# Attention's score matmuls: from one sub-head at a time to both sub-heads in turn

## The reference, cut to what matters

```
def one_block(qblk):                                # 128 queries
    s = einsum('bqhad,bkhad->bhaqk', qblk, k) * scale   # a: sub-head 0 or 1, d: 64 features
    p = softmax(s, axis=-1)
    a = p[:, :, 0] - lam * p[:, :, 1]
    return einsum('bhqk,bkhv->bqhv', a, v)
```

## Time and profile before

| | us |
|---|---|
| median of 3 runs | 3460.33 |
| span of the profiled execution, first to last instruction | 3460.0 |
| PE busy in it | 3105.3 (90%) |
| DVE busy | 1429.9 (41%) |
| ACT busy | 847.0 (24%) |
| attention's first score matmul / last take_o | 339.69 / 723.09 |

### The profile page before, as it was taken

The page is one execution under the profiler, slowest core; times in us unless marked ns, Lnnn a source line. Parts: engine busy times, 40 slices in busy tenths (PEclk is TensorE's granted clock), DMA queues, the critical chain, the costliest instruction groups (busy, mean ns, idle before and its releaser), DMA issues. The chain is left out here.

```text
span 3460.0 us, 42215 instructions
## 1 busy us (share of the span) xinstructions
PE 3105.3 (90%) x16350; PEld 2915.4 (84%) x16350; DVE 1429.9 (41%) x3053; ACT 847.0 (24%) x1041; POOL 747.3 (22%) x250
## 2 busy tenths in 40 slices
PE   5897889869699999999959996999779999999995
PEld 4897666649699999999949994788669999999995
DVE  4677555537523232323343335553462223232325
ACT  3301333340611111111050003552242111111113
POOL 1443000031422112112041111221233211221120
PEclk9998666689899999999979997666889999999997
DMA  5232000023111011101024332110411111111101
GB/s 206 80 119 93 0 1 0 0 100 116 73 42 56 36 36 48 36 36 36 0 113 146 120 133 96 48 47 20 146 43 74 37 48 36 39 57 37 36 12 55
DMA packets 54898, 212.86 MB, mean 62 GB/s; under 512 B 6001, under 2 KB 18993, under 8 KB 45489
## 3 DMA queue, kind: packets, MB, share of 16 engines
q1 hardware_dynamic: 52240, 203.61, 16.4%
q10 hardware_dynamic: 2592, 8.38, 0.6%
HBM read 186.80 MB, written 25.17 MB: 61 GB/s over the span
## 5 line engine op out<-in xcount | busy, mean ns | idle before, releaser
L579 PE MATMUL ps<-hh,wi_hi 128*128 128x384 f32 x2112 | 708.9, 336 | 9.2 <-POOL hl L403 4.9
L581 PE MATMUL ps<-hh,wi_lo 128*128 128x384 f32 x2112 | 708.2, 335 | 0.0
L580 PE MATMUL ps<-hl,wi_hi 128*128 128x384 f32 x2112 | 708.1, 335 | 0.0
L579 PE MATMUL ps<-hh,whi 128*128 128x384 f32 x1344 | 459.6, 342 | 59.6 <-POOL wlo L692 33.3
L961 DVE TENSOR_TENSOR hid<-ps,hid 128x384 f32<-128x384 f32 x132 | 73.4, 558 | 1047.0 <-ACT hid L871 1017.7
L580 PE MATMUL ps<-hl,whi 128*128 128x384 f32 x1344 | 457.1, 340 | 0.0
L581 PE MATMUL ps<-hh,wlo 128*128 128x384 f32 x1344 | 456.6, 340 | 0.0
L579 PEld LDWEIGHTS ps<-hh,wi_hi 128*128 128x128 f32 x2112 | 398.6, 189 | 12.9 <-POOL hl L403 5.7
L580 PEld LDWEIGHTS ps<-hl,wi_hi 128*128 128x128 f32 x2112 | 398.5, 189 | 0.0
L581 PEld LDWEIGHTS ps<-hh,wi_lo 128*128 128x128 f32 x2112 | 398.4, 189 | 0.0
L951 DVE SCALAR_TENSOR_TENSOR x<-ps,mod,x 128x128 f32<-128x128 f32 (+1 forms) x704 | 327.3, 513 | 77.6 <-PE ps L581 72.9
(11 more groups left out here) (174 smaller groups left out, 3999.9 us busy)
## 6 DMA issues: line engine op xcount, KB each, us to landing
raw_in<-in_w_ffn_in_dram SPq DMA_DIRECT2D x44, 1024.0 KB, 4.8
wmt<-in_w_mod_t_dram SPq DMA_DIRECT2D x80, 512.0 KB, 3.5
raw_out<-in_w_ffn_out_dram SPq DMA_DIRECT2D x22, 1024.0 KB, 4.7
gla_spill<-turn SPq DMA_DIRECT2D x24, 576.0 KB, 3.0
head<-gla_spill SPq DMA_DIRECT2D x12, 1152.0 KB, 6.7
raw<-in_w_in_odd_dram SPq DMA_DIRECT2D x24, 512.0 KB, 3.7
raw<-in_w_in_even_dram SPq DMA_DIRECT2D x16, 512.0 KB, 5.6
wm<-in_w_mod_dram SPq DMA_DIRECT2D x12, 512.0 KB, 9.1
```

Source lines behind the costliest of these rows:

```text
L579: pe.matmul(acc, w_hi, in_hi, start=first, stop=False)
L580: pe.matmul(acc, w_hi, in_lo, start=False, stop=False)
L581: return pe.matmul(acc, w_lo, in_hi, start=False, stop=last)
```

## The change

PE's order alone is changed. The 18 score matmuls of a block stand together, chunk by chunk and part by part, alternating between sub-head 0 (partitions 0 to 63) and sub-head 1 (64 to 127). They begin when both sub-heads' exponentials of the block before are made, and `scored` goes up by two behind the last. The values and then all three rounds of transposes follow. Nothing is added or left out: each block has the same 18 score matmuls, 9 transposes, maxima, exponentials and copies.

```
-                def scores(i, u, a):
+                def scores(i, u):
...
-                    wait(pe, exped, i, H2, 2 * (u - 1) + a + 1)
+                    wait(pe, exped, i, H2, 2 * u)
                     for c, cols in enumerate(keys):
-                        acc = ps[:, 3 * a + c, 0:cols.stop - cols.start]
-                        pe.matmul(acc, q_hi[rows, q], k_hi[rows, cols], start=True, stop=False)
-                        pe.matmul(acc, q_hi[rows, q], k_lo[rows, cols], start=False, stop=False)
-                        mm = pe.matmul(acc, q_lo[rows, q], k_hi[rows, cols], start=False, stop=True)
-                    mm.then_inc(scored, 1)
+                        for part, (a_q, a_k) in enumerate(((q_hi, k_hi), (q_hi, k_lo), (q_lo, k_hi))):
+                            for a in range(2):
+                                rows = slice(a * DH, (a + 1) * DH)
+                                mm = pe.matmul(ps[:, 3 * a + c, 0:cols.stop - cols.start], a_q[rows, q], a_k[rows, cols],
+                                               start=part == 0, stop=part == 2)
+                    mm.then_inc(scored, 2)
...
-                    scores(i, 0, 0)
-                    scores(i, 0, 1)
+                    scores(i, 0)
...
-                        scores(i, u, 0)
+                        scores(i, u)
                         if u in (3, 7):
                             values(i, outs)
                             outs += 1
                         if u >= 2:
-                            turning(i, u - 2, outs, (0, 1))
-                        scores(i, u, 1)
-                        if u >= 2:
-                            turning(i, u - 2, outs, (2,))
+                            turning(i, u - 2, outs)
```

More of the change, by code:

```diff
@@ L1211, in _ @@
             def _(pe):
-                def scores(i, u, a):
+                def scores(i, u):
                     q = slice(u * QB, (u + 1) * QB)
                     keys = [slice(0, CTX)] if u == 0 else [slice(CTX + c * CW, CTX + (c + 1) * CW) for c in range(NC)]
-                    rows = slice(a * DH, (a + 1) * DH)
-                    wait(pe, exped, i, H2, 2 * (u - 1) + a + 1)
+                    wait(pe, exped, i, H2, 2 * u)
                     for c, cols in enumerate(keys):
-                        acc = ps[:, 3 * a + c, 0:cols.stop - cols.start]
-                        pe.matmul(acc, q_hi[rows, q], k_hi[rows, cols], start=True, stop=False)
-                        pe.matmul(acc, q_hi[rows, q], k_lo[rows, cols], start=False, stop=False)
-                        mm = pe.matmul(acc, q_lo[rows, q], k_hi[rows, cols], start=False, stop=True)
-                    mm.then_inc(scored, 1)
+                        for part, (a_q, a_k) in enumerate(((q_hi, k_hi), (q_hi, k_lo), (q_lo, k_hi))):
[4 more added lines that the diff above has]
+                    mm.then_inc(scored, 2)
                 def turning(i, u, outs, rounds=range(3)):
```

## The result

| | before | after |
|---|---|---|
| median, us | 3443.59 (9 runs, 3441.3 to 3463.33) | 3485.98 (9 runs, 3467.14 to 3493.76) |
| span of the profiled execution | 3460.0 | 3488.4 |
| ratio to before, 95% interval | | 1.0088 (1.0067 to 1.0110) |

A forecast was written before the change was run, and what follows sets the result against it. PE was taken as the fullest engine of attention, mostly at 1.2 GHz. Longer gaps and paired bursts made +8.6 us a head, +34 over four heads, put onto the median 3460.33: 3495 us, 1.0% slower, range 3474 to 3512.

The forecast's parts named there:

- the sum: Attention's gaps and score bursts from block 1 to 8: 74.80 us against 66.61, with block 1's delay +8.6 a head.
- The chain: Steady blocks: maximum, combine, second maximum and exponentials stand in a row between score bursts, 6.69 us.
- this very order as a rival: DVE combines the block before while scores run: 2.6 of 6.69 us go, 62 us in all, 3433 us; chance near nothing (0.01 with anything else).
- The pairs: Score matmuls of the two sub-heads run side by side: 18 take 3.40 us at 1.2 GHz, 1.86 at 2.4 GHz.
- +34: Attention over four heads, in us: +8.6 a head, with no other stage changed.
- The steady block: Attention blocks in steady state: 6.69 + 3.40 = 10.09 us in place of 8.65.
- Blocks 1 to 3: From scores' end to the next scores: 5.09 us in block 1, 6.69 in a steady block, 7.75 in block 3.
- Block 7: Block with value matmuls: 12.6 us to the next scores (between 11.7 and 13.5), then block 8's scores 2.2 (1.86 to 3.40).
- A sign that missed: DVE idle some 3.4 us before each first maximum, released by PE, and not idle before the second.
- The clock: PE's clock in attention, the open term: low, near 0.5, for the scores of blocks 2 to 7.
- The rival: Clock goes up and stays: steady block 8.55 us, -8 us in all, 3452 us; chance 0.07.
- The transposes' place: PE's nine transposes behind the scores fit beside the wait, over about 4.3 us after the scores' end.

The follow-up runs named there:

- e3: The changed kernel with combine of block u moved on DVE ahead of the first maximum of block u+1: 3429.62 us, ratio 0.9933.
- e6: The changed kernel with combine first on DVE and, on ACT, the copy of round 1 behind the second exponentials: 3423.02 us, ratio 0.9896.
- e1: The kernel before with only values and transposes moved behind both sub-heads' scores; separate waits, no alternation: 3440.74 us, ratio 0.9966.
- e4: The changed kernel with the three transposes of each block's last round made four times: 3479.64 us, ratio 1.0082.
- e2: The changed kernel without alternation, its 18 score matmuls in two runs of nine, joint wait kept: 3533.39 us, ratio 1.0236.

## Why the prediction was right or wrong

**Where it failed, in short.** The mechanism was right, and so was the size of the wait. Two terms of the sum were wrong: the time that it started from ("so the sum goes onto the median", 3460.33 of three runs, where nine runs give 3443.59), and the last pair of each burst (0.67 us, measured 0.52), which made every burst 3.40 us and not 3.24.

**The chain: right, and the cause.** 6.69 us were forecast from the scores' end to the next scores; 6.70 are in the trace. That it was the cause is shown by e3, which takes combine out of it and nothing else: attention falls from 433.7 to 377.9 us. The prediction had this very order as a rival ("If it did, 2.6 us of 6.69 would go", 62 us, 3433). Written as e3 it gives 55.8 us of attention: 1.94 us in a steady block and not 2.6. ACT's two copies then stand in the way; behind one of them alone a block is another 0.4 us shorter (e6).

**The pairs: right in kind, 0.16 us too long.** The step "0.49 + 7 x 0.32 + 0.67 = 3.40" took its last pair from a seam where one stream had joined the other late, so that the merged row's 0.67 holds a lag of about 0.15. In a burst that alternates from the start both halves begin together, and the last row is 0.52: 0.48 + 7 x 0.32 + 0.52 = 3.24. Six bursts a head and four heads make 24 x 0.16 = 3.8 us, as much as the whole difference between +34 and +30.6; what else was off about cancelled. The steady block was forecast at 10.09 and is 9.95.

**Blocks 1 to 3: right.** Block 1 to 2 took 8.34 us (8.49 forecast), 2 to 3 9.94 (10.09), 3 to 4 10.86 (11.15), the first two off by the burst's length. The third is off by 0.29: the burst, and a chain of 7.61 us (467.30 to 474.91) where 7.75 was forecast.

**Block 7: right on average, by luck.** Forecast 12.6 + 2.2 = 14.8 us, each the choice of a value between two bounds. The four heads took 15.82, 16.14, 13.46 and 13.32, mean 14.7, and none came within 1 us of it. In heads 0 and 1 PE began block 8's scores 12.6 and 13.0 us after the end of block 7's, and they took 3.25 and 3.13 us, at the low clock; in heads 2 and 3 they began after 11.6 and 11.5 us and took 1.84, at the high one.

**A sign that missed.** DVE was to be idle some 3.4 us before each first maximum; in steady blocks it was 4.69. Between its second maximum and the next scores stand the second exponentials too, 1.4 us in which DVE has nothing to do. The forecast time doesn't hang on it.

**The clock: right in the blocks, and a term of its own.** Scores of full-row pairs did not bring the clock to their own bursts: 0.50 over three steady blocks. Nor did idle time keep it down before: in e1 PE was busy 21.0 of 21 us, from 462 to 483, at 0.50. The rival is not empty, though. e4 has bursts at 2.4 GHz and blocks of 8.53 to 8.56 us, next to the 8.55 worked out for it.

**The transposes' place.** I priced it at nothing in the change, since it lay beside the chain. Without the joint wait it is a gain, since the two streams then touch in every block, in three pairs and in one by turns (e1). I had the rows for it, 0.32 us from pair to pair where the streams touched, and did not ask what it would do without the wait.

**The time itself: the start was wrong.** The sum was put onto 3460.33, a median of three runs; over nine it is 3443.59. Measured were 3485.98, 9 us below the forecast 3495, and the ratio of 1.0088 on 3443.59 would be 3474, 21 us below it. The step itself is better measured by the ratio, 1.0088 against 1.0100 forecast. That the profiled span lay close to that first median did not make the median safe: all of them were from one group. Beside this, the rounding of +8.54 a head to 8.6 is small, 0.2 us in all.

## What to carry to other kernels

When a change makes one engine's work shorter by making it wait for both halves of a buffer, add up everything the other engines do between release and refill, in their queue's order; that sum then stands between two bursts in full. Here it was 6.7 us, and what it was paid for was 3.3 us of scores (two runs of 3.25 us became one of 3.24). Then move on those engines what need not stand in the sum: with one line moved on DVE and one on ACT, the kernel was 1.0% faster than before, where the change alone had cost 0.9%. And before a forecast is put onto a median of few runs, look whether the runs fall in groups.

## What the runs showed of the hardware

- Matmuls on rows 0 to 63 and on rows 64 to 127, with separate PSUM banks, run fully side by side for nine pairs in a row: 0.32 us a pair at 1.2 GHz, 0.17 at 2.4 GHz, which is the price of one. Each of the 18 has its own weight load, and none shows.
- Without alternation PE pairs at most three matmuls of one half with the first three of the other: three in e2 and in every other block of e1, one in e1's blocks between, and the second of two streams joins with a lag. In e2 the second stream's first matmul (0.69 us long, as the first of a stream is) starts at 480.94 in the trace, ahead of the first stream's seventh at 481.25, although three of the first stream stand before it in the program. Which row is which I infer from their lengths and distances.
- In e4, repeated full-row transposes in otherwise idle time brought the clock to 1.00 for some bursts and not for others in like blocks; which ones I can't say from the traces.
- A difference as large as that between the two groups of runs stands in the gated linear attention stage. The same 1360 matmuls took PE 284.6 us in a stretch of 325 in the profiled run of before, at a mean clock of 0.66, and 266.5 in one of 307 in that of e3, at 0.71, though the code there is the same. Of the nine traces only that of e3 is short there: between the first and the last start of one group of its matmuls (`a_t,v_tok`, 144) lie 238.0 us, in the other eight 252.8 to 254.4. That this makes the two groups is likely, but not shown, since no trace of a run of before from the lower group was kept; and what decides between the two is open:

```profile
2102.00:2427.00 325.00, 284.58 (x1360) 232.70 (x1360) 158.98 (x226) 135.27 (x143) 68.51 (x23) 0.66 0.14 50
```

```profile
2078.00:2385.00 307.00, 266.48 (x1360) 214.43 (x1360) 158.97 (x226) 134.85 (x143) 68.56 (x23) 0.71 0.15 53
```
